# Two norms between a feed-forward layer and its successor: the second root mean square from three sums over f and the old x, x's update on GpSimd

## The reference, cut to what matters

```python
def rms_norm(x, g):
    xf = x.astype(jnp.float32)
    y = xf * lax.rsqrt(jnp.mean(xf * xf, axis=-1, keepdims=True) + RMS_EPS)
    return (y * g.astype(jnp.float32)).astype(x.dtype)
...
        f = conv_glu_ffn(rms_norm(x, ffn_pre_g[layer]), ffn_w_in[layer], ffn_conv_w[layer],
                         ffn_conv_b[layer], ffn_w_out[layer])
        x = x + rms_norm(f, ffn_post_g[layer])
    return x
```

## Time and profile before

| | us |
|---|---|
| median of three runs | 2474.82 |
| lowest and highest of them | 2468.84, 2475.71 |
| profiled execution, its own time | 2469.95 |
| its span, first to last instruction | 2468.2 |
| TensorE busy in it | 2333.1 (95%) |
| VectorE busy | 1495.5 (61%) |
| ScalarE busy | 1096.6 (44%) |
| GpSimd busy | 453.3 (18%) |
| mean granted TensorE clock | 0.976 of full speed |

### The profile page before, as it was taken

How to read it: one execution, slowest core, us unless ns; L and a number is a source line. 1 busy time by engine, 2 the same in 40 slices (tenths; PEclk the granted TensorE clock), 3 DMA queues, 4 the chain that set the end, 5 groups by cost and what they waited for, 6 DMA issues and landing times.

```text
span 2468.2 us, 34942 instructions
## 1 busy us (share of the span) xinstructions
PE 2333.1 (95%) x12834; PEld 1962.2 (79%) x12834; DVE 1495.5 (61%) x2173; ACT 1096.6 (44%) x1768; POOL 453.3 (18%) x448
## 2 busy tenths in 40 slices
PE   8999998888889999879798999999999999999998
PEld 8788887766788788768588888888877778988887
DVE  5785688857578868768935433436757762642433
ACT  5653553535555334543245322325457862431331
POOL 0120122323322212134510000010014431000001
PEclk9999999899999999989999999999999999999999
DMA  5355542222235555334222222222221112222222
GB/s 204 136 187 182 184 176 105 86 69 72 100 121 192 173 167 185 149 144 161 91 77 79 101 102 86 101 87 90 93 86 36 54 53 102 102 85 102 102 85 69
DMA packets 56349, 282.52 MB, mean 114 GB/s; under 512 B 7996, under 2 KB 19008, under 8 KB 28336
## 3 DMA queue, kind: packets, MB, share of 16 engines
q1 hardware_dynamic: 34144, 213.85, 23.9%
q0 software_dynamic: 12560, 58.80, 6.9%
q10 hardware_dynamic: 9536, 8.39, 1.0%
HBM read 265.15 MB, written 15.86 MB: 114 GB/s over the span
## 4 chain that ended last, share of the span: by engine, by line
PE 79%; DVE 14%; ACT 3%; issue 2%; POOL 1%; DMA 1%; SPq 0%; DVEq 0%; ACTq 0%; POOLq 0%
PE ps L481 23%; PE ps L482 22%; PE ps L483 22%; DVE w_lo L1876 3%; PE ps L1031 1%; PE ps L1033 1%; PE ps L1032 1%; PE ps L1071 1%; DVE tg L1941 1%; DVE v L2518 1%; ACT w_hi L1145 1%; POOL sqsum L2818 1%; PE ps L810 1%; PE ps L1087 1%; DVE small L2117 1%
## 5 line engine op out<-in xcount | busy, mean ns | idle before, releaser
L481 PE MATMUL ps<-h_hi,w_hi 128*128 128x512 f32 (+1 forms) x2016 | 742.1, 368 | 26.7 <-DVE w_lo L1876 12.1
L1876 DVE TENSOR_TENSOR w_lo<-raw,w_hi 128x1024 fp32r<-128x1024 f32 x386 | 500.2, 1337 | 415.3 <-ACT w_hi L1145 414.9
L482 PE MATMUL ps<-h_lo,w_hi 128*128 128x512 f32 (+1 forms) x2016 | 732.3, 363 | 0.0
L483 PE MATMUL ps<-h_hi,w_lo 128*128 128x512 f32 (+1 forms) x2016 | 731.8, 363 | 0.0
L1145 ACT ACTIVATE w_hi<-raw 128x1024 fp32r<-128x1024 f32 x386 | 386.7, 1052 | 407.8 <-PE ps L483 405.9
L481 PEld LDWEIGHTS ps<-h_hi,w_hi 128*128 128x128 f32 x2016 | 387.6, 192 | 92.8 <-issue 15.6
L481 PE MATMUL ps<-a_hi,w_hi 128*128 128x512 f32 (+1 forms) x1164 | 424.0, 364 | 20.1 <-DVE f L2334 11.3
L482 PEld LDWEIGHTS ps<-h_lo,w_hi 128*128 128x128 f32 x2016 | 388.1, 192 | 57.5 <-issue 1.0
L483 PEld LDWEIGHTS ps<-h_hi,w_lo 128*128 128x128 f32 x2016 | 387.8, 192 | 57.3
L482 PE MATMUL ps<-a_lo,w_hi 128*128 128x512 f32 (+1 forms) x1164 | 421.5, 362 | 0.0
L483 PE MATMUL ps<-a_hi,w_lo 128*128 128x512 f32 (+1 forms) x1164 | 421.2, 362 | 0.0
(11 more groups left out here) (395 smaller groups left out, 2708.1 us busy)
## 6 DMA issues: line engine op xcount, KB each, us to landing
raw<-weights_dram SPq DMA_DIRECT2D x161, 1024.0 KB, 4.8
ada_w<-ada_dram POOLq DMA_DIRECT2D x48, 1024.0 KB, 5.1
raw<-weights_dram SPq DMA_DIRECT2D x32, 704.0 KB, 3.9
par<-par_dram SPq DMA_DIRECT2D x8, 1152.0 KB, 7.6
par_dram<-plane POOLq DMA_DIRECT2D x10, 512.0 KB, 3.8
tab<-tab_dram SPq DMA_DIRECT2D x8, 512.0 KB, 5.7
x_tok<-x_rows_dram SPq DMA_DIRECT2D x4, 512.0 KB, 6.7
x<-x_in_dram SPq DMA_DIRECT2D x1, 2048.0 KB, 14.6
```

The source lines that it names most:

```text
L481: nc.tensor.matmul(dst, w_hi[:, o:o + P], rhs_hi, start=start, stop=False)
L482: nc.tensor.matmul(dst, w_hi[:, o:o + P], rhs_lo, start=False, stop=False)
L483: return nc.tensor.matmul(dst, w_lo[:, o:o + P], rhs_hi, start=False, stop=last)
L1876: nc.vector.tensor_tensor(w_lo[:, o], raw[:, o], w_hi[:, o].bitcast(f32), SUB).then_inc(w_split, 1)
```

## The change

In both feed-forward layers:

- VectorE's step in `ffn{layer}_out_b` adds the tile's product first, then forms `fx = f * gain * x` (`f_by_x`, new), and splits the weights behind that.
- ScalarE squares each chunk of f twice, plain and with ffn_post's gain (`joint_squares`). GpSimd adds three quantities per chunk (`joint_adds`): sum of f squared, of fx, and of (gain f) squared, where it added one.
- TensorE sums the three over the partitions inside the last half tiles (`joint_sum`). The mean square of the new x is then worked out on 128 x 2 columns (`x1_mean`): r*(r*mean(gf^2) + 2*mean(fx)) + mean(x^2), with r the first norm's reciprocal root and mean(x^2) taken back from the reciprocal root of the norm before. So the squares of the new x, their adds and the second sum go.
- x + f is done by GpSimd (`add_x`); VectorE only scales f (`scaled_f`).
- The orders are new: scaled f, scaled x (`normed`) and low parts (`lows`) of different chunks are interleaved, and the sums and spreads of half 1 lie inside the next phase (`joint_in`, `joint_last`).
- The first spread goes to PSUM bank 7; the first two s5_in tiles swap their banks.

The core of the diff:

```diff
+    def post_spread(h):
+        return bank(POST_AT, TH, off=h * TH)
...
+        def joint_sum(layer, h, q):
+            if q == "fx":
+                pe.wait_ge(sq_added, joint_step(layer, "fx", 7, h))
+            else:
+                pe.wait_ge(sq_added, joint_step(layer, "gsq", 6, h))
+                pe.wait_ge(sq_ready, SQUARES_AT[layer] + 15 + 4 * h + (q == "gsq"))
...
+        def joint_out(layer):
+            return {(0, 1, 4): lambda: joint_sum(layer, 0, "sq"), (0, 1, 5): lambda: joint_sum(layer, 0, "fx"), (0, 1, 6): lambda: joint_sum(layer, 0, "gsq"),
+                    (0, 1, 8): lambda: joint_spread(0, True), (1, 1, 3): lambda: joint_spread(0, False)}
+        def joint_in(layer):
+            return {(0, 0, 3): lambda: joint_sum(layer, 1, "sq"), (0, 0, 4): lambda: (joint_sum(layer, 1, "fx"), joint_sum(layer, 1, "gsq")),
+                    (0, 0, 6): lambda: joint_spread(1, True)}
...
                 if n == 1 and h == 0:
-                    sum_of[1]()
+                    joint_last()
...
+        def second_norm(layer, f_free, eps, dst, shift=None):
+            f_free(0)
+            joint_squares(layer, 6, 0)
+            f_free(0)
+            joint_squares(layer, 7, 0)
+            joint_std(layer, 0, True, eps)
+            joint_std(layer, 0, False, eps)
+            f_free(1)
+            joint_squares(layer, 6, 1)
             split_hi()
-            norm_std(eps, 0)
-            x_halves(1, 0, 1, 2)
-            split_halves(0, range(DC), dst, shift)
+            split_halves(0, range(4), dst, shift)
+            f_free(1)
+            joint_squares(layer, 7, 1)
...
+            def x1_mean(h):
...
+                chain(nc.vector.tensor_tensor(x1_ms[:, b], sums("gsq"), r_post[:, b], MUL))
+                chain(nc.vector.scalar_tensor_tensor(x1_ms[:, b], sums("fx"), 2.0, x1_ms[:, b], MUL, ADD))
+                chain(nc.vector.tensor_tensor(x1_ms[:, b], x1_ms[:, b], r_post[:, b], MUL))
+                chain(nc.vector.tensor_tensor(x1_ms[:, b], x1_ms[:, b], x_ms[:, b], ADD))
+                nc.vector.tensor_scalar(x1_ms[:, b], x1_ms[:, b], 0.0, None, MAX).then_inc(rstd_ready, 1)
...
             f_half(0, 0)
             f_half(1, 0)
+            post_rstd(0)
+            x1_mean(0)
             rstd_on_all()
+            scaled_f(0, 0)
+            pre_rstd(0)
+            scaled_f(0, 1, 2)
             f_half(0, 1)
+            scaled_f(0, 3)
             split_lo()
             rstd_on_all()
+            normed(0, 0)
+            scaled_f(0, 4)
+            normed(0, 1)
+            lows(0, 0)
+            f_half(1, 1)
+            scaled_f(0, 5)
+            normed(0, 2)
+            lows(0, 1)
...
+            lows(0, 4)
+            post_rstd(1)
+            x1_mean(1)
+            normed(0, 6)
+            lows(0, 5)
             rstd_on_all()
+            scaled_f(1, 0)
+            normed(0, 7)
+            lows(0, 6)
+            pre_rstd(1)
+            scaled_f(1, 1)
+            lows(0, 7)
             split_lo()
+            scaled_f(1, 2)
             rstd_on_all()
+            for c in range(DC + 1):
+                if c < DC:
+                    normed(1, c)
+                if c + 3 < DC:
+                    scaled_f(1, c + 3)
+                if c:
+                    lows(1, c - 1)
...
                 d = chunk(f, out_chunk.now())
-                nc.vector.tensor_tensor(d, d, bank(2 * u), ADD).then_inc(acc_free["dve"], 1)
+                ins = nc.vector.tensor_tensor(d, d, bank(2 * u), ADD)
+                ins.then_inc(acc_free["dve"], 1)
+                f_by_x(out_chunk.n)
                 out_chunk.after()
...
+                fx_at[layer, c, h] = mark(nc.vector.scalar_tensor_tensor(view(fx, c % 2), view(f, c), post(c), view(x, c), MUL, MUL))
...
+                    chain(nc.vector.tensor_tensor(x_ms[:, :], rcol[:, :], rcol[:, :], MUL))
+                    chain(nc.vector.reciprocal(x_ms[:, :], x_ms[:, :]))
+                    chain(nc.vector.tensor_scalar(x_ms[:, :], x_ms[:, :], EPS_A, None, SUB))
-                    tiles(f"ffn{layer}_out_b", add_out, (out_chunk, 1), then=more_turns5 if layer else constants5, last=2)
+                    tiles(f"ffn{layer}_out_b", add_out, (out_chunk, 1), splits="last", then=more_turns5 if layer else constants5, last=2)
...
+            for c in range(6):
+                for q in ("sq", "fx", "gsq"):
+                    add_one(q, c)
+            for q in ("sq", "fx", "gsq"):
+                add_one(q, 6, 0)
+            add_one("fx", 7, 0)
+            add_x(0, 0, 1, 2, 3)
+            for q in ("sq", "fx", "gsq"):
+                add_one(q, 6, 1)
+            add_x(0, 4, 5)
+            add_one("fx", 7, 1)
+            add_x(0, 6, 7)
+            add_x(1, *range(DC))
```

More of the change, by code:

```diff
@@ L128, in norm_adds_table, with joint_step @@
     return table
+JOINT = ([(q, c, None) for c in range(6) for q in ("sq", "fx", "gsq")] + [("sq", 6, 0), ("fx", 6, 0), ("gsq", 6, 0), ("fx", 7, 0)]
+         + [("x", c, 0) for c in range(4)] + [("sq", 6, 1), ("fx", 6, 1), ("gsq", 6, 1)] + [("x", 4, 0), ("x", 5, 0), ("fx", 7, 1), ("x", 6, 0), ("x", 7, 0)]
+         + [("x", c, 1) for c in range(8)])
+JOINT_AT = (0, len(JOINT) + 32)
+SQUARES_AT = (0, 20 + 32)
+def joint_step(layer, q, c, h=None):
+    return JOINT_AT[layer] + JOINT.index((q, c, h)) + 1
 ADDS = norm_adds_table()
@@ L224, in build @@
     q = f
+    gsq, fx = place("gsq", 2 * T, offset=H0 + 8 * KB), place("fx", 2 * T, offset=H0 + 12 * KB)
+    fx_sum, gsq_sum = place("fx_sum", T, offset=H0 + 28 * KB), place("gsq_sum", T, offset=H0 + 30 * KB)
+    x_ms, r_post, x1_ms = (place(n, NB, offset=W0 + 5 * KB + 192 + 32 * k) for k, n in enumerate(("x_ms", "r_post", "x1_ms")))
+    COLS = {"sq": 0, "fx": 4, "gsq": 8}
+    SUM_OF = {"sq": sqsum, "fx": fx_sum, "gsq": gsq_sum}
+    POST_AT, ready_before = 7, {}
+    SUM_AT = {(q, h): 6 if q == "sq" else 4 + h for q in COLS for h in range(2)}
     small = place("small", 32 * 32, offset=W0)
@@ L664, in ffn @@
             phase(f"ffn{layer}_out_b", FH, 1, a_hi, a_lo, a_ready, ab + FH, last=2)
-            out_pair(f"ffn{layer}_out_b", FH, 1, a_hi, a_lo, {(0, 1, 7): sum_of[0], (1, 1, 3): spread_of[0]})
-            second_norm()
+            out_pair(f"ffn{layer}_out_b", FH, 1, a_hi, a_lo, joint_out(layer))
+            ready_before[layer] = C["spread"].n
         def rope_pair():
@@ L1393, in squares, with f_free @@
                 act.wait_ge(acc_free["dve"], C["free_dve"].after())
-                square(chunk(f, out_chunk.now()), chunk(sq, (u + FIRST[f"ffn{layer}_out_b"]) % 2))
+                joint_squares(layer, out_chunk.n)
                 out_chunk.after()
-            def f_half(t, h):
+            def f_free(h):
                 if h:
@@ L1450, in ffn @@
                 else:
-                    tiles(f"ffn{layer}_out_b", squares, (out_chunk, 1), (C["free_dve"], 1), (C["sq"], 1), then=tables5 if layer else rope_sines, last=2)
+                    tiles(f"ffn{layer}_out_b", squares, (out_chunk, 1), (C["free_dve"], 1), then=tables5 if layer else rope_sines, last=2)
             if layer:
-                second_norm(f_half, EPS_B, h_hi, lambda c: mod[:, c:c + 1])
+                second_norm(1, f_free, EPS_B, h_hi, lambda c: mod[:, c:c + 1])
             else:
-                second_norm(f_half, EPS_A, a_hi)
+                second_norm(0, f_free, EPS_A, a_hi)
         ffn(0)
@@ L1993, in second_norm @@
+            C["norm"].after(4)
+            C["lo"].after(2 * DC)
+            C["hp"].after(2 * DC)
             g.after(2)
@@ L2329, in ffn @@
             out_chunk = Count()
+            post = lambda c: v("ffn_post", 8 * layer + c)
             def add_out(u):
@@ L2831, in add_halves, with joint_adds, add_one, add_x @@
                 add(halved(sqsum, 0, h), halved(sq, c % 2, h))
[L2833 to L2850 removed]
+        def joint_adds(layer):
+            at = JOINT_AT[layer]
+            gp.wait_ge(norm_sum_done, C["norm"].n)
+            gp.wait_ge(tile_done, tile_at(FIRST[f"ffn{layer}_out_b"]))
+            gp.memset(sqsum[:, :], 0.0)
+            gp.memset(fx_sum[:, :], 0.0)
+            gp.memset(gsq_sum[:, :], 0.0).then_inc(sq_zero, 1)
+            gp.wait_ge(sq_zero, C["zero"].after())
+            def add_one(q, c, h=None):
+                view = (lambda t, k: chunk(t, k)) if h is None else (lambda t, k: halved(t, k, h))
+                if q == "fx":
+                    gp.wait_ge(dve_step, fx_at[layer, c, h])
+                else:
+                    before = 2 * c if h is None else 12 + 2 * (c - 6) + 4 * h
+                    gp.wait_ge(sq_ready, SQUARES_AT[layer] + before + (2 if q == "gsq" else 1))
+                last = joint_step(layer, q, c, h) - 1
+                if last > at:
+                    gp.wait_ge(sq_added, last)
+                dst = view(SUM_OF[q], 0)
+                gp.tensor_tensor(dst, dst, view({"sq": sq, "fx": fx, "gsq": gsq}[q], c % 2), ADD).then_inc(sq_added, 1)
```

(10 more changed lines are left out.)

162 lines of the change are left out of this document (99 added, 63 removed).

## The result

The changed kernel takes 2490.27 us (median of 4 runs, 2486.79 to 2492.04), the kernel before on the same chip 2471.94 (4 runs). The ratio is 1.0068 with a 95% interval of 1.0052 to 1.0085: slower by 13 to 21 us. Its profiled execution has a span of 2487.9 us, 19.7 more than before.

A forecast was written before the change was run, and what follows sets the result against it. TensorE, 95% busy, bounds the kernel, but VectorE sets layer 0's T. 15.2 - 8.1 + 1.4 + 1.0 - 6.1 = +3.4 us on the profiled 2469.95, 2473.4; 2478 as a median; range 2463 to 2493.

The forecast's parts named there:

- likeliest case: Whole kernel: no change within 0.3%, chance 0.45; the likeliest case by itself was 2471 to 2486 us.
- a low clock in the out-projection: Rival, layer 0's out-projection: waits lower TensorE's clock, tiles take more than 9.7 us, 2486 in all; chance 0.2.
- a hole that moves: Rival, behind the out-projection: tile 8's split and GpSimd's x adds delay the first low part, +10 us, 2488; chance 0.1.
- T: Start of t1 half 0 in the out-projection, 414.04 us in layer 0 before; predicted 15.2 us later there.
- marker to T: From the 0.80 us low-part wait at the out-projection's start to t1 half 0's start; T predicted 15.2 us later, layer 0.
- x_ms: Three chained small VectorE operations added in layer 0's out-projection, 0.22 us each, 0.7 in all.
- The rival with the cheap lock: Out-projection: added GpSimd adds cost VectorE little, under 0.4 us each; 2467, or 2457 with low parts keeping pace; chance 0.18.
- The 1.9 charged at T: Layer 0, t1 half 0: 1.9 us added for the lower clock level after a wait of some 8 us.
- The hole: TensorE's idle stretch behind the out-projection, before the first low part: predicted 3.5 us instead of 15.
- Behind T, layer 0: From t1 half 0 to the query projection: 8.1 us shorter than 60.1, then +1.4 query norm and +1.0 lower clocks.
- the walk: VectorE's queue followed operation by operation behind t1 half 0: half 1 starts at T+36.6, values end at T+52.0.
- Layer 1: T from 1062.8 to about 1063.8, s5_in tiles ending 7.1 us earlier, +1.0 for clocks: -6.1 us.

The follow-up runs named there:

- before_add_first: The kernel before with the add of the tile's product ahead of the split of the weights in both out-projections; 2465.13 us, one run.
- before_extra_adds: The kernel before with two more 512-column GpSimd adds on scratch behind each of six whole-chunk adds of both out-projections; 2484.05 us, one run.
- filler run: The changed kernel with 60 extra unread matmuls per transition ahead of the first half's chunks behind both out-projections; 2484.38 us, ratio 1.0047 to the kernel before.
- no_read_adds: The changed kernel with GpSimd's adds of fx and of the squared-gain sum for chunks 0 to 5 replaced by memsets; 2472.09 us, one run.
- early: The changed kernel with the S5 constants moved to the first half of layer 0's out-projection; 2474.89 us, ratio 1.0010 to the kernel before.

## Why the prediction was right or wrong

The time, 2490, lies in the range of 2463 to 2493 and outside the likeliest case's own 2471 to 2486, and it is slower (0.68%), which had a chance of 0.37, where "within 0.3%" was likeliest. The sum was +3.4; the trace has +19.7. That the time is inside the range is luck: its upper part was there for a low clock in the out-projection and a hole that moves, and neither brought it.

**Ahead of T, layer 0: right.** I said 15.2 us, and marker to T went from 45.4 to 60.6. The parts are right as well: before_add_first gives -0.8 for the order (said: -1.14), before_extra_adds +10.6 for the adds (said: 11.0), which leaves 5.4 for x_ms and six fx (said: 0.7 and 4.7). The rival with the cheap lock is refuted. The waits of 2 to 4 us in front of each tile were partly there (2.97, 3.70, 0.20, 1.69), with 7.05 at T.

**The clock in the out-projection: right to leave out, but close.** The rival had the clock fall in these tiles; it was granted 0.96 there. Behind the wait of 3.70 it did fall (0.74 from 396 to 400, 0.84 in the next four), behind that of 2.97 it didn't. That tile took 9.6 us (396.76 to 406.34, with 0.20 of waiting), just short of the rival's 9.7, so VectorE stayed the bound. The 1.9 charged at T was spent: the window from 427 to 443 has 0.84, which is 5.1 us at the lower level or 2.6 us lost.

**The hole: right.** I said 3.5 us, its end at T+18.6; it was 2.84, its end at T+20.3. The rival in which the hole only moves gives about the measured time, but its mechanism did not happen.

**Behind T, layer 0: wrong, and this is the step that failed.** The prediction has 60.1 - 8.1 + 1.4 + 1.0 = 54.4 us from T to the query projection (its list of signs says 52, which leaves the last two terms out); it was 62.6. The place where it went off is the walk between the hole and the spread of half 1, predicted from T+18.6 to T+36.6 and measured from T+20.3 to T+45.9. Two terms:

- "For lower clocks in a stretch with so many short waits I add 1.0 (bounds 0 and 1.9)." At least 5.4 us in layer 0 and 5.2 in layer 1 by the filler run, far above the upper bound. I had priced a low clock only by the work that it slows for a moment behind one long wait. Here it stayed for 23 us, slowed the sums to 4 us, and VectorE, the pacemaker of the walk, stood waiting for them. Then the value block took 5.3 us to the spread instead of 3.0.
- Ahead of that spread the walk never let VectorE wait for TensorE. In the filler run, at the full clock, it does for 4.1 us. The spread of half 1 comes at T+40.6 in the filler run: my 36.6 and these 4.1. That this explains it is worked out from the waits, not tried by another order, and the extra matmuls are a part of the 4.1.

The last leg, spread to query projection, was right: 16.6 us, where I had 15.4 and 1.4 for the query norm.

**Layer 1: T right for wrong reasons, the rest wrong.** I said that T comes 1.0 later from the marker; it was 0.9 (53.5 to 54.4). But the order alone brings the kernel before to 44.1 (T at 1055.1, worked out as 33 matmuls of 0.12 behind t0's start at 1051.14, and no wait), and the new norm takes it back to 54.4, 8.1 of it by the added adds (no_read_adds: 46.3). I had believed that 1.73 us of slack in each step would swallow most of the locks; most of the slack was only there because of the ring that the order opens, and with it gone VectorE, which has no idle time from 1032.5 to T, is the bound as in layer 0. Behind T the gain failed for the same two terms (3.47 and 2.25 us of waits there, 2.28 and 1.69 in the filler run): B grew by 3.0 where -6.1 was expected.

**"I would be wrong most of all in T of layer 0"** was wrong too. I had widened the range where the row was good (one add per step, 1.13) and trusted the walk, which no row had shown.

## What to carry to other kernels

Work moved to GpSimd isn't free for a VectorE that has no idle time: count each GpSimd add that reads SBUF as its own duration on VectorE, unless it falls beside VectorE's reads of PSUM or where VectorE waits anyway, and compare that with doing the work there. When one engine is to be fed by another chunk by chunk, walk both queues with the waits in both directions, and walk it a second time at TensorE's lower clock. Give the kernel before every side effect of the change (here the order of add and split, worth 6.4 us in layer 1) before the change gets the credit or the blame. And when work is moved to a place with slack, measure that place too: the constants cost 3.7 us where VectorE was busy for half the time.

## What the runs showed of the hardware

- The clock fell after small things. In the changed kernel TensorE waited 2.84 us, did six matmuls of 0.12, waited 1.36, and was then at the lower level until about 473, busy for 21.73 of 25.7 us. In early it fell behind a wait of 1.20 us and 20 one-column matmuls that stand among products, with TensorE counted busy for 6.00 of 6.00 us in the window where it was low. With 14 extra matmuls at that place it stayed at 1.00.
- At the lower level the 20 one-column matmuls of the second half's sums took 4.0 us (452.59 to 454.15 and 455.57 to 457.99), at the higher one 2.1 (456.46 to 457.27 and 458.77 to 460.03 in the filler run): the small steps of a chain slow down with the clock as products do.
- VectorE and GpSimd slow each other: a GpSimd add of 512 columns takes 1.27 us beside chains and 2.07 to 2.36 beside a split of weights, while it takes 1.0 to 1.1 from VectorE in either case. A `TENSOR_SCALAR` of 128 x 512 with one SBUF input takes 0.43 alone and 1.40 with an add beside it. GpSimd's memsets, which read nothing, cost VectorE nothing that shows: the split at 395.16 in no_read_adds, with an add and two memsets of 128 x 512 beside it, takes 3.46, and the same split in before_add_first (1040.37), with one add alone, 3.46.
